# Two weight forms of the seven-product down projection trade half slots, and the raw panel's slot is given back at the earlier one

## What is computed

```
h = modulate(rms_norm(x, norm_g[layer, 1]), sh2, sc2)
x = x + g2[:, None, :] * (jnp.square(jax.nn.relu(h @ w_ff1[layer])) @ w_ff2[layer])
```

## Time and profile before

| what | value |
|---|---|
| median of 3 runs | 1349.97 us |
| lowest, highest | 1349.79, 1349.97 us |
| the profiled execution, its own time | 1350.72 us |
| span of its instructions | 1349.0 us |
| PE busy | 1311.5 us, 97% |
| DVE busy | 792.4 us, 59% |
| ACT busy | 535.5 us, 40% |
| POOL busy | 292.1 us, 22% |
| granted clock of PE, mean | 0.996 of full |

### The profile page before, as it was taken

How to read it: one execution, slowest core, us unless ns; L and a number is a source line. 1 busy time by engine, 2 the same in 40 slices (tenths; PEclk the granted TensorE clock), 3 DMA queues, 4 the chain that set the end, 5 groups by cost and what they waited for, 6 DMA issues and landing times.

```text
span 1349.0 us, 26219 instructions
## 1 busy us (share of the span) xinstructions
PE 1311.5 (97%) x10430; PEld 1221.7 (91%) x10430; DVE 792.4 (59%) x1447; ACT 535.5 (40%) x968; POOL 292.1 (22%) x334
## 2 busy tenths in 40 slices
PE   8899999998999999999999999999999999999997
PEld 6789877777888988998999999999999999999997
DVE  3534332665655647956854653667566588687365
ACT  3433332544333424534433331324344354453354
POOL 4200153961310203403400210003001023141000
PEclk9999999999999999999999999999999999999999
DMA  9977686214664446264252232213223213324242
GB/s 336 376 257 247 229 288 243 91 63 155 221 219 156 156 160 210 82 205 157 71 182 77 94 94 63 68 63 94 94 63 120 84 63 103 98 81 126 80 139 98
DMA packets 128834, 195.97 MB, mean 145 GB/s; under 512 B 5885, under 2 KB 104714, under 8 KB 125653
## 3 DMA queue, kind: packets, MB, share of 16 engines
...
...
## 4 chain that ended last, share of the span: by engine, by line
PE 89%; DVE 4%; issue 2%; DMA 2%; ACT 2%; POOL 1%; POOLq 0%; DVEq 0%; SPq 0%; ACTq 0%
PE gemm L1983 63%; PE gemm L2429 10%; PE gemm L2400 3%; PE aux_ps L2018 2%; PE gemm L2138 2%; DVE w_lo L1639 1%; PE stat_ps L2150 1%; PE aux_ps L2186 1%; PE stat_ps L2087 1%; PE stat_ps L2328 1%; ACT P L1039 1%; DMA v_third<-in_cache_v 1%; PE aux_ps L2068 1%; DMA ada_w<-in_w_ada 1%; PE gemm L2287 1%
## 5 line engine op out<-in xcount | busy, mean ns | idle before, releaser
L1983 PE MATMUL gemm<-h_split,w_hi 128*128 128x272 f32 (+1 forms) x3328 | 568.9, 293 | 4.4 <-DVE h_split L1277 1.9
L1983 PEld LDWEIGHTS gemm<-h_split,w_hi 128*128 128x128 f32 x3328 | 469.8, 189 | 43.8 <-issue 35.3
L1983 PE MATMUL gemm<-h_split,w_lo 128*128 128x272 f32 (+1 forms) x1664 | 346.2, 289 | 0.0
L1983 PEld LDWEIGHTS gemm<-h_split,w_lo 128*128 128x128 f32 x1664 | 262.7, 188 | 0.0
L1208 DVE TENSOR_TENSOR w_lo<-raw_panels,w_hi 128x1024 fp32r<-128x1024 f32 x160 | 195.2, 1222 | 110.6 <-ACT w_hi L711 109.4
L711 ACT ACTIVATE w_hi<-raw_panels 128x1024 fp32r<-128x1024 f32 x160 | 168.0, 1052 | 166.4 <-PE gemm L1983 149.2
L1983 PE MATMUL gemm<-hid_split,w_hi 128*128 128x272 f32 x1024 | 170.6, 288 | 0.0
L1983 PEld LDWEIGHTS gemm<-hid_split,w_hi 128*128 128x128 f32 x1024 | 144.7, 188 | 0.0
L1983 PE MATMUL gemm<-hid_split,w_lo 128*128 128x272 f32 x512 | 105.8, 288 | 0.0
L2429 PE MATMUL gemm<-hid_t,w_hi 128*128 128x272 f32 x512 | 97.9, 288 | 3.7 <-DVE c_sum L1710 3.7
L661 POOL TENSOR_TENSOR w_sum<-raw_panels 128x512 f32<-128x512 f32 x32 | 51.1, 1597 | 173.1 <-DMA raw_panels<-in_w_ff 112.7
...
## 6 DMA issues: line engine op xcount, KB each, us to landing
raw_panels<-in_w_ff SPq DMA_DIRECT2D x68, 1024.0 KB, 5.4
ada_w<-in_w_ada POOLq DMA_DIRECT2D x36, 1024.0 KB, 5.9
...
raw_panels<-in_w_in_ab SPq DMA_DIRECT2D x12, 1024.0 KB, 10.0
...
raw_panels<-in_w_in_c SPq DMA_DIRECT2D x8, 1024.0 KB, 5.4
...
```

The costliest lines, as they stand in the source:

```text
L1983: ins = mm(G[slot][:, 512 - T0W * (1 - half):512 + (T0W + rows) * half], w[:, s, k, :], rhs(k, part, T0W * half, T0W + rows * half), start ...
```

## The change

Forms 5 and 6 trade half slots: form 6, the last raw quarter, goes into half slot 5 and form 5 into half slot 6. For pair 0 the order in which ACT and DVE make these two is traded as well. So form 6 of pair 0 is made in the last up unit beside form 4, and form 5 in `fast_down` where form 6 was. For pairs 1 to 3 the order stays. The function `form_count` gives the count that `lo_done` and `hi_done` reach with form 5 or 6 of a pair; for pair 0 it is now one earlier for form 6 and one later for form 5. The waits follow:
- The load for pair 2 waits for form 6 of pair 0 only, and for the four additions of pair 0, which read the panel too. The load for pair 3 keeps its count.
- POOL's addition k = 3 of pair 1 waits for form 5 of pair 0, in its new place.
- Behind the last pair the split of the third next unit goes into slot 2, which form 6's half slot is part of. On ACT it now waits for the pair's last product, and on DVE it comes behind `add_samples`.
- SP's loop over the four blocks is unrolled, and in the fast blocks so are the four loads of w_ff2.

```
--- before.py
+++ after.py
@@ -346,7 +346,15 @@
 
         def w_part(buf, k):
 
-            return buf[:, k // 2, 4 * (k % 2):4 * (k % 2) + 4, :]
+            h = HALF_SLOT[k]
+            return buf[:, h // 2, 4 * (h % 2):4 * (h % 2) + 4, :]
+
+        HALF_SLOT = (0, 1, 2, 3, 4, 6, 5)
+        FORM_ORDER = ((0, 1, 2, 3, 4, 6, 5),) + 3 * ((0, 1, 2, 3, 4, 5, 6),)
+
+        def form_count(n, k):
+
+            return PAIR_T[n] + FORM_ORDER[n % 4].index(k) - 4
 
         W_RAW = {0: (0, 0), 3: (1, 0), 6: (1, 1)}
         W_SUM = {1: 0, 2: 1, 4: 2, 5: 3}
@@ -439,11 +447,21 @@
             two_panels(14, panel["out_ab"], 512)
 
             def load_ff(layer, p0):
-                with sp.Fori(0, 4) as b:
+                for b in range(4):
                     with sp.Fori(0, 2) as i:
                         two_panels(p0 + 8 * b + 2 * i, ff1_v[layer], 1024 * b + 512 * i)
-                    with sp.Fori(0, 2) as i:
-                        two_panels(p0 + 8 * b + 4 + 2 * i, ff2_v[layer], 512 * i, rows=KC * b)
+                    if b not in FAST:
+                        with sp.Fori(0, 2) as i:
+                            two_panels(p0 + 8 * b + 4 + 2 * i, ff2_v[layer], 512 * i, rows=KC * b)
+                        continue
+                    for j in range(4):
+                        n, p = 4 * fast_ix(layer, b) + j, p0 + 8 * b + 4 + j
+                        if j < 2:
+                            sp.wait_ge(lo_done, 2 * p - 2)
+                        else:
+                            sp.wait_ge(lo_done, form_count(n - 2, 6))
+                            sp.wait_ge(ws_add, WS_ADD0 + 4 * (n - 2) + 4)
+                        sp.dma_start(raw[:, j % 2, :, :], ff2_v[layer][:, KC * b:KC * b + KC, 256 * j:256 * j + 256]).then_inc(raw_in[j % 2], 16)
 
             load_ff(0, T_FF0 // 2)
             for part, col in ((0, D), (4, 0)):
@@ -647,7 +665,7 @@
                 if n and k < 3:
                     pool.wait_ge(lo_form, LO_FORM0 + 5 * (n - 1) + (2, 3, 5)[k])
                 if n and k == 3:
-                    pool.wait_ge(lo_done, PAIR_T[n - 1] + 1)
+                    pool.wait_ge(lo_done, form_count(n - 1, 5))
                 if k == 0:
                     terms = w_quarter(raw, p, 0, 1), w_quarter(raw, p, 1, 1)
                 elif k == 1:
@@ -737,7 +755,7 @@
                 n, t = 4 * B + j, PAIR_T[4 * B + j]
                 p = t // 2
                 if j == 0:
-                    act.wait_ge(unit_done, UD0 + t - 3 + k // 2)
+                    act.wait_ge(unit_done, UD0 + t - 3 + HALF_SLOT[k] // 2)
                 elif k < 5:
                     act.wait_ge(prod, PROD0 + 5 * (n - 1) + k + 1)
                 else:
@@ -787,8 +805,8 @@
                     if s < 5:
                         split_hi(ahead(t // 4, t % 4))
                     else:
-                        form_hi(B, 0, 2 * (s - 5))
-                        form_hi(B, 0, 2 * (s - 5) + 1)
+                        form_hi(B, 0, FORM_ORDER[0][2 * (s - 5)])
+                        form_hi(B, 0, FORM_ORDER[0][2 * (s - 5) + 1])
                     act.wait_ge(unit_done, UD0 + t + 1)
                     act.wait_ge(psum_free, t + 2)
                     A(rel[:, 0, :], gall[s % 2], ACT.Relu).then_inc(relu_r, 1)
@@ -831,7 +849,7 @@
                 hid_t3_hi(4 * B + 3, 3)
                 hid_t4_hi(4 * B + 3, 3)
                 keep_u2(0)
-                form_hi(B, 0, 6)
+                form_hi(B, 0, 5)
                 for k in range(7):
                     form_hi(B, 1, k)
                 for j in range(1, 3):
@@ -849,6 +867,7 @@
                 keep_u2(3)
                 act.wait_ge(prod, PROD0 + 5 * n + 4)
                 split_next(u + 1)
+                act.wait_ge(unit_done, UD0 + u)
                 split_next(u + 2)
 
             def step_none(q, s):
@@ -1634,7 +1653,7 @@
                 if k < 5:
                     dve.wait_ge(hi_form, HI_FORM0 + 5 * n + k + 1)
                 else:
-                    dve.wait_ge(hi_done, t + k - 4)
+                    dve.wait_ge(hi_done, form_count(n, k))
                 src = w_quarter(raw, p, *W_RAW[k]) if k in W_RAW else w_sum[:, W_SUM[k], :, :]
                 V.tensor_tensor(w_part(w_lo, k), src, w_part(w_hi, k).bitcast(f32),
                                 ALU.subtract).then_inc(lo_form if k < 5 else lo_done, 1)
@@ -1665,8 +1684,8 @@
                     if s < 5:
                         split_lo(ahead(t // 4, t % 4))
                     else:
-                        form_lo(B, 0, 2 * (s - 5))
-                        form_lo(B, 0, 2 * (s - 5) + 1)
+                        form_lo(B, 0, FORM_ORDER[0][2 * (s - 5)])
+                        form_lo(B, 0, FORM_ORDER[0][2 * (s - 5) + 1])
                     dve.wait_ge(relu_r, 32 * layer + 8 * b + s + 1)
                     if Q:
                         dve.wait_ge(t_add, T_ADD0 + 4 * Q)
@@ -1746,7 +1765,7 @@
                     split_lo((u // 4, u % 4))
 
                 u = PAIR_T[4 * B] + 8
-                form_lo(B, 0, 6)
+                form_lo(B, 0, 5)
                 add_c11(0)
                 if layer == 0:
                     ada_turn(3 + b)
@@ -1783,10 +1802,10 @@
                 split_next(u + 1)
                 add_c22(3)
                 sum_c12(3)
-                split_next(u + 2)
                 add_c12(3)
                 add_c21(3)
                 add_samples(3)
+                split_next(u + 2)
 
             def part_resid(t, ps, m, r, gate):
 
@@ -2409,7 +2428,7 @@
                         if k < 5:
                             pe.wait_ge(lo_form, LO_FORM0 + 5 * n + k + 1)
                         else:
-                            pe.wait_ge(lo_done, t + k - 4)
+                            pe.wait_ge(lo_done, form_count(n, k))
                         if k < 2:
                             pe.wait_ge(psum_free, t + 1)
                         if k == 0 and j:
```

10 lines of the change are left out of this document (5 added, 5 removed).

## The result

The changed kernel takes 1358.18 us, median of 4 runs (1357.68 to 1360.65), beside 1349.97 (1349.79 to 1350.42) for the kernel before. The ratio is 1.0064, with a 95% interval of 1.0047 to 1.0081: slower by 8.2 us, where 2.15 had been forecast and 1356.3 was the end of the range.

A forecast was written before the change was run, and what follows sets the result against it. PE, busy 97%, was taken to bound the kernel, its waits in `fast_down` being for late DVE. Stretch terms 0.4 + 0.4 + 0 + 1.35 = +2.15 us on 1349.97 gave 1352.1 us, range 1347.0 to 1356.3.

The forecast's parts named there:

- Part 1, the trade: Forms 5 and 6 of pair 0: form 5 made 6.3 us into pair 0, in time for product 5; cost 0.
- Part 2, the load: Pair 2's load goes out at 1099.2, not 1107.05; pair 2's additions move about 3 us forward, into pair 0.
- Part 3, the added wait: POOL's k = 3 of pair 1 waits for form 5 until 1106.79, so it too falls into pair 0.
- The sum for pair 0: DVE's steps in pair 0, held by three additions: 2.9 us lost in stretches 3 and 4, 2.65 in the first layer.
- So the 2.6 us of pair 1 go: Pair 1, relieved of additions, loses its waits: -1.4, -2.7, -2.6 and -2.6 us in the four stretches.
- Pair 2's own price: Pair 2, with pair 3's four additions in a row: 0.1 us a stretch, bounded by 0 and 1.0.
- Part 4, the end of the stretch and SP: Split of the third next unit behind the last pair, and SP's unrolled loop: cost 0.
- cleared: Rival: pair 2's additions find room in pair 0, only k = 3 costs; -5.7 us, 1344.3 us; chance 0.10.
- nothing: Rival: the additions were not what held DVE, so no change, 1350.0 us; chance 0.08.
- Turns fall out better: Rival: in pair 0 POOL's k = 1 of pair 2 runs only behind form 3; -1.0 us, 1349.0 us; chance 0.18.
- Pair 2 is hit as well: Rival: pair 3's additions hold DVE before `sum_c22` of pair 2, up to 1.0 a stretch; 1355.8 us; chance 0.17.

The follow-up runs named there:

- small additions: Changed kernel and kernel before, each with additions of pairs 1 to 3 cut to 16 columns of one chunk: ratios to before 0.9924 and 0.9955.
- late load: Changed kernel, but pair 2's load again waits for both forms 5 and 6 of pair 0: ratio to before 1.0001.
- the longer wait with PE idle and with PE kept busy: Changed kernel plus three DVE additions ahead of `sum_c12` of pair 0, without and with 32 filler transposes on PE: 1368.1 and 1358.8 us, one execution each.
- the repeats: Changed kernel run again unaltered: ratio to before 1.0052, then a third time, one execution, 1357.7 us.

## Why the prediction was wrong

- *Part 1, the trade:* right. Form 5's low part ended 6.3 us into pair 0 (1110.28) and nothing waited for it; the small additions show the edit at 0.
- *Part 2, the load:* right. Issued 1102.43, 1.5 us before the stretch. The first addition of pair 2 then waited for form 1 of pair 1, as forecast, and moved into pair 0.
- *Part 3, the added wait:* right in its place, 6.4 us into the pair. Alone it costs 0.8 us, measured with the late load.
- *The sum for pair 0:* right. Forecast 13.35 us for the third stretch and 13.5 for the first layer, measured 13.36 and 13.46 to 13.48. In all four +11.1 forecast, +11.06 measured.
- *"So the 2.6 us of pair 1 go":* this step failed, by 5.5 us. It took 9.3 out of pair 1, and 3.83 went. 3.1 of the miss is the clock. The prediction counted only how long PE waits, and put nothing for the clock that PE is granted behind a wait of this length: it cost 1.5 us in each of two stretches, and the longer wait with PE idle and with PE kept busy shows the cause. A row of the trace of before could have warned of it, at the start of the output projection, where PE waited 3.08 us. The same wait stands in all eighteen profiled executions, and the clock fell at it in seventeen. Here that row and the window behind it:

```profile
314.75 0.59 PE L1983 MATMUL gemm<-mix_hi,w_hi 128*128 128x272 f32 x2 [3.08 <-DVE mix_lo L1624]
```

```profile
314.80:318.30 3.50, 3.50 (x16) 3.50 (x17) 3.50 (x6) 2.06 (x4) 1.06 (x2) 0.52 0.47 180
```

- The other 2.3 or so of the miss lie ahead of pair 2, 1.0, 0.5 and 0.7 us in stretches 2 to 4. The prediction let DVE finish `sum_c12` before pair 3's additions begin, both 22.8 us into the stretch. In the third they began 22.3 us in, at 1126.28, 0.06 before `add_c22` (L1734), which then took 1.53 us:

```profile
1125.73 0.69 DVE L1658 TENSOR_TENSOR w_lo<-w_sum,w_hi 128x512 fp32r<-128x512 f32 x1 [0.22 <-ACT w_hi L769]
1126.34 1.53 DVE L1734 SCALAR_TENSOR_TENSOR x_resid<-c_sum,gate_pm,x_resid 128x240 f32<-128x240 f32 x1
1127.79 0.43 DVE L1741 TENSOR_TENSOR c_sum<-gemm,p_cp 128x272 f32<-128x272 f32 x1
```

  In the first stretch they began half a microsecond later in it, behind the start of `add_c22`, which took 0.46. `sum_c12` ended 23.3 us in, and PE did not wait. So a few tenths in the landing of pair 3's load decide this wait. POOL, then DVE:

```profile
564.49 1.31 POOL L679 TENSOR_TENSOR w_sum<-raw_panels 128x512 f32<-128x512 f32 x1 [4.32 <-DMA raw_panels<-in_w_ff]
...
564.14 0.46 DVE L1734 SCALAR_TENSOR_TENSOR x_resid<-c_sum,gate_pm,x_resid 128x240 f32<-128x240 f32 x1
564.52 0.43 DVE L1741 TENSOR_TENSOR c_sum<-gemm,p_cp 128x272 f32<-128x272 f32 x1
```

  A part of the 2.3 goes back to the clock as well: behind a fall PE waited 0.78 and 0.50 us there, and 0.33 to 0.35 in those stretches of the repeats in which it waited without a fall.

- *Pair 2's own price*, 0.1 a stretch: it was about 0, and -0.25 in the first stretch. The forecast of 0.4 in all was 0.7 too high.
- *Part 4, the end of the stretch and SP:* right, 0. The gaps between the stretches did not move.
- The sum: +11.06 - 3.83 - 0.26 = +7.0 in the profile. The medians are 8.2 apart; the 1.2 between is not told apart from the spread of the runs.
- *The rivals:* "cleared" and "nothing" are out. "Turns fall out better" is out too: k = 1 of pair 2 ran ahead of form 3's low part. "Pair 2 is hit as well" came nearest in time, 1355.8, and the sign that it named came (pair 3's additions began before DVE was through with `add_c12` of pair 1), but its cost did not: they struck at the end of pair 1, and pair 2 did not grow. That its time is near is luck, as it counts nothing for the clock.
- The Trainium skill's rule on the shared port (SBUF — State Buffer, Who interferes with whom) is borne out: with the additions cut to 16 columns the low parts are back at 0.69 us and none of the waits that the change brought is left. In pair 0 each of the three stretched low parts ends 0.55 us behind the addition that it meets (1112.21 behind 1111.66, 1114.81 behind 1114.26, 1116.86 behind 1116.31), so DVE waits each addition out. By the rule with three additions met at their start it would lose 3.9 us; the steps worked out from the rows of before put `sum_c12` 3.0 us later, and it came 3.04 later.
